# Layer norms done one token tile at a time, with the next layer's first units behind them, and five weight slots

## What is computed

```python
for i in range(DEPTH_2):                       # 2 layers
    if i < N_A_LAYERS:                         # layer 0
        mix = ssd_mixer(h, ...)                # h4; out_proj: "so"
    else:                                      # layer 1
        mix = mla_attention(h, ...)            # h6; out_proj: "ao"
    h = layer_norm(DN_ALPHA * h + mix, ln_mix_g[i], ln_mix_b[i])
    ff = conv_ffn(h, ...)                      # h5 and h7: up, conv of 3 taps, silu * val, down
    h = layer_norm(DN_ALPHA * h + ff, ln_ffn_g[i], ln_ffn_b[i])
```

```python
def layer_norm(x, g, b):
    xf = x.astype(jnp.float32)
    mu = jnp.mean(xf, axis=-1, keepdims=True)
    var = jnp.mean(jnp.square(xf - mu), axis=-1, keepdims=True)
    return ((xf - mu) * lax.rsqrt(var + LN_EPS) * g.astype(jnp.float32) + b.astype(jnp.float32)).astype(x.dtype)

def conv_ffn(h, up, conv_w, conv_b, down):
    u = causal_depthwise_conv(h @ up, conv_w, conv_b)
    g, val = jnp.split(u, 2, axis=-1)
    return (jax.nn.silu(g) * val) @ down
```

## Time and profile before

| | us |
|---|---|
| median of 3 runs | 1368.99 |
| lowest and highest run | 1368.66 and 1370.35 |
| profiled execution | 1367.49 |
| its span, first to last instruction | 1365.7 |
| PE busy in the span | 1301.1 |
| DVE busy | 887.6 |
| ACT busy | 676.3 |
| mean TensorE clock granted, share of full | 0.981 |

### The profile page before, as it was taken

The page is one execution under the profiler, slowest core; times in us unless marked ns, Lnnn a source line. Parts: engine busy times, 40 slices in busy tenths (PEclk is TensorE's granted clock), DMA queues, the critical chain, the costliest instruction groups (busy, mean ns, idle before and its releaser), DMA issues.

```text
span 1365.7 us, 19955 instructions
## 1 busy us (share of the span) xinstructions
PE 1301.1 (95%) x8527; PEld 1182.8 (87%) x8527; DVE 887.6 (65%) x1166; ACT 676.3 (50%) x832; POOL 51.7 (4%) x62
## 2 busy tenths in 40 slices
PE   6999999999999999989999997999998898999997
PEld 6878999988979999989987776999997866899996
DVE  5666757874545444478867768666667646766666
ACT  3654533534435445446664443555553453555552
POOL 4000000110000000000000001000001000000000
PEclk9999999999999999999999998999998999899998
DMA  9544546665435555555542235555553423355551
GB/s 335 165 127 145 168 155 200 206 196 176 138 124 185 185 186 185 159 191 173 176 154 93 93 116 165 182 185 185 185 185 118 161 92 117 120 188 188 188 187 63
DMA packets 155352, 223.28 MB, mean 163 GB/s; under 512 B 4997, under 2 KB 117361, under 8 KB 155008
## 3 DMA queue, kind: packets, MB, share of 16 engines
q1 hardware_dynamic: 151936, 210.38, 47.7%
q0 software_dynamic: 3040, 11.04, 2.2%
q10 hardware_dynamic: 288, 0.59, 0.1%
...
## 4 chain that ended last, share of the span: by engine, by line
PE 85%; DVE 8%; ACT 3%; issue 2%; DMA 1%; POOL 1%; DVEq 0%; SPq 0%; ACTq 0%
PE bank L1720 26%; PE bank L1721 26%; PE bank L1722 26%; DVE bn L1135 1%; ACT whi L684 1%; DMA raw<-in_w_in 1%; DVE xn L1133 1%; DVE xn L1146 1%; POOL rstd L601 1%; DVE xn L1157 1%; DVE wlo L1045 1%; DVE h_lo L1057 1%; PE bank L1950 1%; ACT arena L701 1%; PE bank L2090 1%
## 5 line engine op out<-in xcount | busy, mean ns | idle before, releaser
L1045 DVE TENSOR_TENSOR wlo<-raw,whi 128x2048 fp32r<-128x2048 f32 (+2 forms) x203 | 455.5, 2249 | 165.3 <-ACT whi L684 164.8
L1720 PE MATMUL bank<-h_hi,whi 128*128 128x256 f32 x1632 | 467.3, 286 | 8.3 <-DVE h_lo L1057 7.2
L1721 PE MATMUL bank<-h_lo,whi 128*128 128x256 f32 x1632 | 464.9, 285 | 0.0
L1722 PE MATMUL bank<-h_hi,wlo 128*128 128x256 f32 x1632 | 464.8, 285 | 0.0
L684 ACT ACTIVATE whi<-raw 128x2048 fp32r<-128x2048 f32 (+2 forms) x203 | 381.9, 1884 | 102.6 <-DMA raw<-in_w_up 31.3
L1720 PEld LDWEIGHTS bank<-h_hi,whi 128*128 128x128 f32 x1632 | 316.6, 194 | 12.0 <-issue 7.5
L1721 PEld LDWEIGHTS bank<-h_lo,whi 128*128 128x128 f32 x1632 | 316.6, 194 | 1.3
L1722 PEld LDWEIGHTS bank<-h_hi,wlo 128*128 128x128 f32 x1632 | 316.3, 194 | 0.0
L1720 PE MATMUL bank<-whi,r_hi 128*128 128x512 f32 (+1 forms) x432 | 167.4, 388 | 5.5 <-ACT arena L701 2.1
L1721 PE MATMUL bank<-wlo,r_hi 128*128 128x512 f32 (+1 forms) x432 | 166.6, 386 | 0.0
L1722 PE MATMUL bank<-whi,r_lo 128*128 128x512 f32 (+1 forms) x432 | 166.0, 384 | 0.0
...
## 6 DMA issues: line engine op xcount, KB each, us to landing
...
```

The costliest lines, as they stand in the source:

```text
L1045: V.tensor_tensor(wlo[s][:, 0:kt * n], raw[s][:, 0:kt * n], whi[s][:, 0:kt * n].bitcast(F32), ALU.subtract).then_inc(lo_split, 1)
L1720: M(o, a_hi, b_hi, start=start, stop=False)
L1721: M(o, a_hi, b_lo, start=False, stop=False)
L1722: return M(o, a_lo, b_hi, start=False, stop=stop_)
```

## The change

Four things change together.

1. **Five slots.** `SLOTS` becomes 5. The room comes from `rows`, which has two rows instead of four: the gain and the bias row of a layer norm are loaded into the same two places each time, once the norm before has used them. `ssd_norm_g` becomes a per-channel vector in `pv`, applied when the transposed result is split (ACT and DVE each two operations of 128x256 per bank, where there was one of 128x512); the group norm's four operations lose the gain.
2. **Last pair by tile.** The last two units of `so` and `ao` are computed together by `last_two`: tile 0 in both column halves, then tile 1. The last two down groups of an FFN (`down(9)`, `down(10)`) are joined in `last_two_wide`, behind `up(10)` and `down(8)`. `layer_norm` adds both banks of tile 0 and finishes it, and then does tile 1; in between it makes the low halves of tile 0's transposed x. A bank of transposes is now four channel tiles of one token tile. The first group of tile 0's transposes stands in the last block of the pair.
3. **First units by tile.** FFN unit 0 (both halves) is computed token-major, tile 0 first (`first_half`), into one bank per tile; ACT copies it to `ftN` and `first_back` transposes it back to channel-major, 16 transposes in each FFN. q-down is computed tile by tile as well. The FFN's r parts have four places.
4. **MLA in another order.** The query latent's transposes stand inside kv-down; each q-up unit is a rope part and then a nope part; units 0 and 1 come before the key and value up projections and units 2 and 3 behind; the steps of attention are interleaved with value-up, q-up and the first two units of `ao`, whose input now lies in `r_hi`.

The core of the diff:

```diff
-SLOTS = 4
-G_MLP = 552
+SLOTS = 5
+G_MLP, G_SSD = 552, 560
 UNIT = 2048
...
+def ffn_order():
+    order = [("up", 1), ("down", 0)]
+    for g in range(2, FFN_GROUPS - 1):
+        order += [("up", g), ("down", g - 1)]
+    last = FFN_GROUPS - 1
+    return order[:-1] + [("up", last), ("down", last - 2), ("down", last - 1), ("down", last)]
...
             def ffn_part(layer, g):
                 act.wait_ge(f_prod, 11 * layer + g + 1)
-                A(r_hi[:, 2 * (g % 2):2 * (g % 2) + 2, :], fcv[g % 2][0], ACT.Copy).then_inc(x_hi, 1)
...
+            def tile_part(name, t, c):
+                b = wait_bank(act, (name, t, c))
+                part(h_hi[:, 4 * c:4 * c + 4, P * t:P * t + P], b[:, :].rearrange("p (k t) -> p k t", k=4))
...
                 nc.scalar.preload_act_table_set("silu_and_others")
+                for c in range(2):
+                    tile_part(name, 0, c)
+                hi()
+                tile_part(name, 1, 0)
+                copy_bank(ftN[:, 0, :], ("ft", layer, 0), lambda b: b[:, :])
+                tile_part(name, 1, 1)
+                hi()
+                copy_bank(ftN[:, 1, :], ("ft", layer, 1), lambda b: b[:, :])
...
+            def layer_norm(name, uses, alpha=ALPHA, lo_name=None):
+                def add(c, t):
+                    key, x_ = name(c, t), xn[:, t, halves[c]]
+                    b = wait_bank(dve, key)
+                    V.scalar_tensor_tensor(x_, x_, alpha, b[:, :], ALU.mult, ALU.add).then_inc(done(key), 1)
+                    wait_drained(dve, key)
+                    mark(V.bn_stats(bn[:, t, c, :], x_))
+                def finish(t):
+                    dve.wait_ge(dve_step, steps[0])
+                    mark(V.bn_aggr(mv[:, t, :], bn[:, t, 0:2, :]))
+                    tile_inverse(t, LN_EPS, False)
+                    mark(V.scalar_tensor_tensor(xn[:, t, :], xn[:, t, :], mv[:, t, 0:1], rows[:, 0, :], ALU.subtract, ALU.mult))
+                    wait_inverse(powers[0])
                     dve.wait_ge(dve_step, steps[0])
                     for c in halves:
-                        V.scalar_tensor_tensor(xn[:, t, c], xn[:, t, c], rstd[:, t:t + 1], rows[:, bias[0], c], ALU.mult, ALU.add)\
+                        V.scalar_tensor_tensor(xn[:, t, c], xn[:, t, c], rstd[:, t:t + 1], rows[:, 1, c], ALU.mult, ALU.add)\
                             .then_inc(normed, 1)
+                def tile_lo(t):
+                    for c in range(2):
+                        key, k = (lo_name, t, c), slice(4 * c, 4 * c + 4)
+                        b = wait_bank(dve, key)
+                        part(h_lo[:, k, P * t:P * t + P], b[:, :].rearrange("p (k t) -> p k t", k=4), h_hi[:, k, P * t:P * t + P])\
+                            .then_inc(done(key), 1)
+                for slot in range(2):
+                    dve.wait_ge(row_in[slot], 16 * uses)
+                add(0, 0)
+                add(1, 0)
+                finish(0)
+                add(0, 1)
+                if lo_name is not None:
+                    tile_lo(0)
+                add(1, 1)
+                finish(1)
+                if lo_name is not None:
...
                     for g in range(2):
                         y = yN[q % 2][:, t, 256 * g:256 * g + 256]
-                        V.scalar_tensor_tensor(y, y, rstd[:, 2 * t + g:2 * t + g + 1], gains[:, MIX * q + 256 * g:MIX * q + 256 * g + 256],
-                                               ALU.mult, ALU.mult).then_inc(y_done, 1)
+                        V.tensor_scalar(y, y, rstd[:, 2 * t + g:2 * t + g + 1], None, ALU.mult).then_inc(y_done, 1)
...
             def ffn_part(layer, g, base):
-                s = slice(2 * (g % 2), 2 * (g % 2) + 2)
+                s = slice(2 * (g % 4), 2 * (g % 4) + 2)
...
             ffn_pads()
-            xT_parts("h5", h_lo, h_hi)
             lo()
+            layer_norm(lambda c, t: ("so", c, t), 3, lo_name="h5")
             ffn(0)
-            layer_norm(lambda c, t: ("ffn", 0, c, t), (1, 3), (2, 3))
...
             lo()
+            layer_norm(lambda c, t: ("ffn", 0, c, t), 4, lo_name="h6")
...
+            lo()
+            rope(0)
+            lo()
+            part_bank(r_lo, r_hi, ("latk", 0), slice(4, 6))
+            rope(1)
+            lo()
+            attend(0)
+            lo()
...
+            def last_two(us, x_hi_, x_lo_, tile0, banks, before):
+                for t in range(NT):
+                    for c in range(2):
+                        w_hi, w_lo, kt, n = weights(us[c])
+                        for k in range(kt):
+                            before(t, c, k)
+                            ts = slice(P * t, P * t + P)
+                            last = three(banks[c][t][:, :], x_hi_[:, tile0 + k, ts], x_lo_[:, tile0 + k, ts], w_hi[:, k, :], w_lo[:, k, :],
+                                         False, k == kt - 1)
...
+            def tile_transpose(name, t, c):
+                halves_normed[0] += 1
+                pe.wait_ge(normed, halves_normed[0])
+                b = claim((name, t, c))
+                for k in range(4):
+                    last = nc.tensor.transpose(b[:, P * k:P * k + P], xn[:, t, P * (4 * c + k):P * (4 * c + k) + P], ident)
+                last.then_inc(fill((name, t, c)), 1)
...
+                def before(t, c, k):
+                    if (t, c, k) == (1, 1, 2):
+                        tile_transpose(name, 0, 0)
+                return before
...
+                def first_half(t, c, x):
+                    if (c, x) == (0, 0):
+                        first.append(claim(("ft", layer, t)))
+                    if x == 0:
+                        wait_drained(pe, (name, t, c))
+                    w_hi, w_lo, kt, n = weights(at[("fu", layer, 0, x)])
+                    ts = slice(P * t, P * t + P)
+                    for k in range(4 * c, 4 * c + 4):
+                        last = three(first[t][:, 256 * x:256 * x + 256], h_hi[:, k, ts], h_lo[:, k, ts], w_hi[:, k, :], w_lo[:, k, :],
+                                     (x, k) == (0, 0), (x, k) == (1, kt - 1))
+                    if c == 1 and t == 1:
+                        last.then_inc(unit_used, 1)
+                    elif (c, x) == (1, 1):
+                        last.then_inc(fill(("ft", layer, t)), 1)
...
+                def up_second(j):
+                    if j == 1:
+                        first_back(1)
+                first, back = [], []
+                tile_transpose(name, 0, 1)
+                first_half(0, 0, 0)
+                first_half(0, 0, 1)
+                first_half(0, 1, 0)
+                tile_transpose(name, 1, 0)
+                first_half(0, 1, 1)
+                tile_transpose(name, 1, 1)
+                first_half(1, 0, 0)
+                first_half(1, 0, 1)
+                first_back(0)
+                first_half(1, 1, 0)
+                first_half(1, 1, 1)
+                for n, (what, g) in enumerate(FFN_ORDER):
+                    if what == "up":
...
+                last_two_wide([at[("fd", layer, g)] for g in pair], lambda i: pe.wait_ge(f_lo, 11 * layer + pair[i] + 1), r_hi, r_lo,
+                              [2 * (g % 4) for g in pair], banks, before_last)
+            ffn(0, "h5", first_tile("h6"))
...
+            q_nope_part(0)
+            q_rope_part(1)
+            pe.wait_ge(lat_ready, 5)
```

497 lines of the change are left out of this document (322 added, 175 removed).

## The result

| | before | changed |
|---|---|---|
| median of 4 runs, us | 1369.33 | 1348.20 |
| lowest and highest | 1368.66 and 1370.35 | 1347.42 and 1349.23 |
| span of the profiled execution | 1365.7 | 1346.2 |

The ratio is 0.9845, with a 95% interval of 0.9832 to 0.9859: 21 us or 1.5% less. Measured once more, the changed kernel ran in 1350.12 beside 1369.41 (ratio 0.9859, 0.9846 to 0.9873); of its eight runs the middle is 1348.8. The forecast was 1348.3.

The account below looks back on a forecast made before the run. PE was taken to bound the kernel, busy 1301.1 of 1365.7 us, leaving its idle and low-clock time to win. Gains 2.8+5.8+7.1+2.7+2.3 = 20.7 gave span 1345.0, plus 1.8 and 1.5: 1348.3 us, range 1342 to 1360.

Parts of the forecast that it names:

- The seams: Stretches around the layer norms where PE waits; at h5, 16.0 us from the pair's end to unit 0, against 23.6.
- h5: Seam into the FFN behind SSD: gain 7.6, less 0.5 transposes back, 4.05 weight waits, 0.2 in SSD: net 2.8 us.
- sign of being right: One listed observation that would show the forecast right: full clock through h5 and h7.
- h7: Seam into the FFN behind MLA: gain 7.3 with a first wait of 0.3, less 0.5 and 4.05: 2.7 us.
- h6: Seam before MLA's q-down ends: gain 6.1, plus 1.2 for r_lo's wait, less 1.5 for low clock: 5.8 us.
- MLA: Latent and attention section: 11.2 us of idle time and low clock could go, new waits cost 4.15: gain 7.1.
- End: Program's tail: 10.0 us falls to 7.95, gaining 2.0, plus 0.3 from the last r_lo: 2.3 us.
- Fifth slot: With row loads and a small DMA: no weight's landing is waited for in the bodies, gain 0, bounds -1 and +1.
- Rival 1: Low clock follows the short waits too, 3.4 us more in each seam: 1353 to 1356 us; chance 0.20.
- Rival 2: Waits of a tile each switch the clock low for long, nine places at 4.4 us: slower, 1388; chance 0.06.
- Rival 3: The FFN's start hides its weight splits, two times 2.5 us less: 1343; chance 0.09.
- Rival 4: Splits ahead of the norm on DVE eat tile 0's cover, seams win 1 us at most: about 1368; chance 0.05.

Follow-up runs that it names:

- two_splits: Changed kernel with DVE making the low halves of both up(1) weights ahead of unit 0's taps at each FFN start: 1345.96 us.
- early_mo_split: Changed kernel with the split of the weight of h7's first FFN unit moved ahead of the last attention output's copy: 1348.83 us, again 1346.85.
- first_whole: Changed kernel with FFN unit 0 as before the change, all transposes first, both halves channel-major over 256 tokens, nothing transposed back: 1353.27 us.
- three_splits: As two_splits, with the weight of down(0) also split ahead of the FFN's first terms and taps, on ACT and DVE: 1339.25 us.
- four_slots: Changed kernel with four weight slots instead of five, all else the same: 1363.33 us.

## Why the prediction was right, and where it was not

**The seams and what fills them.** The mechanism came out as told: tile 0's transposes inside the last block, no clock lost through the first unit of h5, unit 0 complete 16 us after the end of the pair's products (from 841.8, the end of the products if the wait and the transposes among them are left out, to 858.1: 16.3; forecast 16.0). Its waits were 0.90 for 0.65 and 0.97 for 0.9; the one of 0.45 for tile 0's low half was 0.13, since DVE begins the first of them (843.06) ahead of the pair's end. One sign of being right did not come: full clock through h5 and h7. The first profile has a stretch at half clock in h5, behind the wait on the weight, and the second has one in h7 as well.

**h5: 2.7 for 2.8.** The first wait on a weight is 2.55 where the chain gave 2.5. The second, 1.55, isn't there, because a stretch at half clock of 3.4 us slowed PE by the same 1.5. In h7, with the clock up, it is there with 1.39, and in two_splits, with the clock up in h5, with 1.99. The size was right and one of its causes wrong.

**h6: 6.8 for 5.8.** The waits are 0.32, 1.09 and 0.87 for 0.3, 1.15 and 0.75. The 1.5 that I had charged for a low stretch wasn't due in this execution; in that of two_splits it was. No run took h6's part back, so its 6.8 is read from the two traces alone.

**MLA: 7.0 for 7.1**, but not with the waits of my list: 1.47 (1.6), 0.56 (0.35), 0.67 and 0.66 (0.85 and 1.1), none for the latents of q (0.25), and one of 1.05 in the output projection that I had not seen. 4.4 in all for 4.15.

**h7: 1.1 for 2.7.** The term that was mis-sized is the first wait, 0.3 in the prediction, for which I gave a reason that belongs to the wide pair of the FFN; the pair ahead of h7 is the one of the output projection. It was 1.80, because the attention's end leaves two splits in DVE's queue ahead of the norm (early_mo_split: 0.26 without one of them). The term was worth 1.5 of the 1.6 that are missing. In h5 as well a split ends just where the norm's first sum begins (835.60), so part of its 0.90 may be of this kind; no run took that one away.

**End: 2.3 for 2.3**: 8.09 of tail for 7.95, and 0.4 ahead of it.

**Fifth slot: the reason that failed.** "Nothing waits for a weight's landing in the bodies: 0, bounds -1 and +1" was read from a kernel in which the norm came behind everything else. In the new order DVE's queue has a split ahead of the norm, and with four slots that split waits for its landing. Without the slot 15 of the 21 us are gone. The slot has no gain of its own in the trace of before; it is what the others need. The one wait that may be its own gain, 0.81 us at 290.66 of before, isn't in the changed kernel and is back with four slots (0.87).

The sum was 20.7 for 19.5, and the forecast met the time to 0.1 only because the median lay 2.0 over the span where 3.3 were added. That is luck, and so is that h6's 1.0 too little and h7's 1.6 too much nearly cancel. **Rival 1** has some truth: short stretches of half clock did follow new waits, 3.4 us in one execution and 10.2 in another, which costs 1.5 to 4.5; they follow waits of over 1 us, and none of 10.2 us in one piece appeared but in first_whole (a wait of 5.6). **Rival 2** is out by the same rows. **Rival 3**, that the FFN's start hides its splits, was wrong of the changed kernel and is what three_splits makes true. **Rival 4** had in it the mechanism that four_slots and h7 show, a split queued ahead of the norm on DVE.
